# The masks of two attention stages added on TensorE, with the work at the ends of the stages in another order

## The reference

```
first block:  h += 0.5*ffn(norm h); h += conv mixer; h += 0.5*ffn;  kv projections of h
              h += 0.5*ffn; h += nsa(norm h) @ w_o; h += 0.5*ffn
   nsa: 16 heads, each with 3 branches (15 compressed keys, 256 selected, 256 in the window),
        softmax(q k^T / 8 + bias), gated and summed
second block: x += rms_norm(even_mixer(rms_norm x)) ; x += rms_norm(odd_mixer(rms_norm x))
   even: 8 heads of width 64 over the 64 best keys of an index score; retention beside it
   odd:  4 differential heads: softmax(q1 k1) - lambda softmax(q2 k2), and 8 latent heads of 96
         s = jnp.where(kpos <= qpos, q k^T * scale, -inf); p = softmax(s); o = p v
   m = concat(...) @ w_out (1024 x 1024); x = x + rms_norm(m, post_norm)
```

## Time and profile before

| | us |
|---|---|
| median of 3 runs | 1430.54 (1428.55 to 1437.21) |
| the profiled execution | 1427.65 |
| its span | 1425.4 |
| PE busy in it | 1305.7 (92%) |
| DVE busy | 889.0 (62%) |
| ACT busy | 619.0 (43%) |
| POOL busy | 438.4 (31%) |
| mean granted clock of PE | 0.961 |

### The profile page before, as it was taken

One profiled execution on the slowest core, in us unless ns is written; L12 is line 12 of the kernel. 1 busy time (PEld: TensorE's weight loads), 2 busy tenths in 40 slices (PEclk: granted clock), 3 DMA queues, 4 the chain that ended last, 5 costly groups with the idle time before them and its releaser, 6 DMA issues.

```text
span 1425.4 us, 27104 instructions
## 1 busy us (share of the span) xinstructions
PE 1305.7 (92%) x10681; PEld 1239.2 (87%) x10681; DVE 889.0 (62%) x1228; ACT 619.0 (43%) x924; POOL 438.4 (31%) x198
## 2 busy tenths in 40 slices
PE   5899999999999998999998778999999997699776
PEld 4899998989999998999996547999999996688665
DVE  3685458786545576454567864754556687674795
ACT  3444335344434445343345674533434445434451
POOL 1345432214443343444410332344340004300042
PEclk9999999999999999999998799999999999999898
DMA  6877754656776455665643103666653460444012
GB/s 195 218 212 218 224 180 134 178 176 203 224 212 204 158 175 173 198 200 178 187 126 101 34 23 115 199 188 191 205 163 107 146 215 31 136 136 150 12 46 73
DMA packets 275097, 222.50 MB, mean 156 GB/s; under 512 B 8082, under 2 KB 256422, under 8 KB 274908
## 3 DMA queue, kind: packets, MB, share of 16 engines
q1 hardware_dynamic: 272528, 215.59, 49.8%
q0 software_dynamic: 1344, 4.46, 1.6%
q10 hardware_dynamic: 1164, 1.62, 0.4%
HBM read 216.40 MB, written 4.19 MB: 155 GB/s over the span
## 4 chain that ended last, share of the span: by engine, by line
PE 72%; DVE 14%; ACT 7%; DMA 3%; issue 3%; POOL 1%; ACTq 0%; DVEq 0%; SPq 0%
PE psum L669 22%; PE psum L671 22%; PE psum L670 22%; DVE wal L1568 2%; ACT pbuf L1378 1%; ACT wah L1156 1%; DVE pbuf L1781 1%; DVE nmx L1783 1%; DVE hnl L1586 1%; POOL wbl L2172 1%; DVE wal L1742 1%; ACT wbh L1163 1%; ACT hnh L1226 1%; DMA raw_a<-in_ffn_w_in 1%; PE psum L632 1%
## 5 line engine op out<-in xcount | busy, mean ns | idle before, releaser
L669 PE MATMUL psum<-hnh,wah 128*128 128x256 f32 (+1 forms) x2080 | 589.9, 284 | 14.3 <-DVE wal L1568 7.7
L670 PE MATMUL psum<-hnl,wah 128*128 128x256 f32 (+1 forms) x2080 | 581.2, 279 | 0.0
L671 PE MATMUL psum<-hnh,wal 128*128 128x256 f32 (+1 forms) x2080 | 580.8, 279 | 0.0
L2172 POOL TENSOR_TENSOR wbl<-raw_b,wbh 128x1024 fp32r<-128x1024 f32 x114 | 369.0, 3238 | 570.6 <-ACT wbh L1163 465.0
L669 PEld LDWEIGHTS psum<-hnh,wah 128*128 128x128 f32 (+1 forms) x2080 | 396.3, 191 | 21.4 <-issue 8.6
L670 PEld LDWEIGHTS psum<-hnl,wah 128*128 128x128 f32 (+1 forms) x2080 | 395.8, 190 | 2.2 <-issue 1.7
L671 PEld LDWEIGHTS psum<-hnh,wal 128*128 128x128 f32 (+1 forms) x2080 | 395.8, 190 | 0.0
L1568 DVE TENSOR_TENSOR wal<-raw_a,wah 128x2048 fp32r<-128x2048 f32 (+1 forms) x129 | 298.0, 2310 | 105.4 <-ACT wah L1156 104.2
L1156 ACT ACTIVATE wah<-raw_a 128x2048 fp32r<-128x2048 f32 (+2 forms) x127 | 238.9, 1884 | 92.7 <-PE psum L671 65.4
L1264 ACT ACTIVATE gate_hid<-tmp 128x256 f32<-128x256 f32 x88 | 36.7, 417 | 421.0 <-DVE tmp L1677 421.0
L669 PE MATMUL psum<-hidh,wbh 128*128 128x256 f32 x768 | 213.3, 278 | 5.3 <-DVE hidl L1622 5.2
(11 more groups left out here) (286 smaller groups left out, 1568.7 us busy)
## 6 DMA issues: line engine op xcount, KB each, us to landing
raw_a<-in_ffn_w_in SPq DMA_DIRECT2D x176, 512.0 KB, 5.1
raw_b<-in_ffn_w_out SPq DMA_DIRECT2D x88, 512.0 KB, 5.0
raw_a<-in_w_in_even SPq DMA_DIRECT2D x15, 1024.0 KB, 5.4
raw_a<-in_conv_w_in SPq DMA_DIRECT2D x24, 512.0 KB, 3.9
raw_a<-in_w_in_odd SPq DMA_DIRECT2D x11, 1024.0 KB, 5.3
raw_a<-in_w_kv SPq DMA_DIRECT2D x6, 1024.0 KB, 6.5
raw_b<-in_conv_w_out SPq DMA_DIRECT2D x8, 512.0 KB, 5.6
raw_a<-in_attn_w_q SPq DMA_DIRECT2D x4, 1024.0 KB, 5.2
```

The source lines that it names most:

```text
L669: mm(dst, wh, xh, start=start, stop=False)
L670: mm(dst, wh, xl, start=False, stop=False)
L671: return mm(dst, wl, xh, start=False, stop=stop)
L2172: g.tensor_tensor(wbl[:, s], raw_b[:, s], wbh[:, s].bitcast(F32), ALU.subtract).then_inc(S("b_lo"), 1)
```

## The change

Masks: causal16, dmask and a 128 x 128 identity are kept in bf16. In even and odd PE first writes the mask into the score banks (identity times mask), then adds q k^T. DVE takes the maxima from PSUM and scales them; ACT takes the exps from PSUM with the scale in the instruction and writes the probabilities. The scores of duo g now wait for the exps of duo g-2. In nsa, ACT copies a unit's high part before the exps of the step, and DVE takes its low part one step later (back = LAG + 3); late_queries runs at steps 6, 9, 12, 15, and PE asks at 12, 15, 18, 21. Low parts of the last output row (even) and the last two (odd) go from POOL to DVE. The Sqrt table load of the even stage is made right after its attention stage, that of the odd stage is gone. DVE adds pairs of squares (half_ready), and PE sums four tiles instead of eight. At the end PE sums hres and the normed output in PSUM, both by a product with the identity, into four banks; ACT copies three of them, DVE one. Cut diff:

```diff
--- before.py
+++ after.py
@@ -148,6 +148,9 @@
         zero = sb("zero", [P, 512], BF16)
+        causal16 = sb("causal16", [P, 384], BF16)
+        dmask = sb("dmask", [P, 384], BF16)
+        ident16 = sb("ident16", [P, P], BF16)
         rms = sb("rms", [P, T + 2])
@@ -342,6 +344,9 @@
+        Y_BANK = (4, 5, 7, 6)
+        POOL_LOWS = {"nsa": 2, "even": 7, "odd": 6}
@@ -467,7 +472,10 @@
                 c = slice(half * 512, (half + 1) * 512)
-                sp.wait_ge(S("y_copied"), j + 1)
+                if j == 2:
+                    sp.wait_ge(S("y_third"), 1)
+                else:
+                    sp.wait_ge(S("y_copied"), min(j + 1, 3))
                 sp.dma_start(out[0, tt * P:(tt + 1) * P, c], xn[:, tt, c]).then_inc(S("y_stored"), 16)
@@ -570,7 +578,7 @@
-                                 bias=dmask[:, None, :].to_broadcast([P, 2, 384]), scale=SQRT_D,
+                                 bias=None, mask=dmask, scale=SQRT_D,
@@ -578,17 +586,16 @@
-            bias = causal[:, None, :].to_broadcast([P, 2, 384])
-                duos.append(dict(kind="full", q=[cq[r, h] for r in rows], k=[ck[r, h] for r in rows], bias=bias,
-                                 scale=SQRT_D, v=[v, v], rows=[slice(0, P)] * 2, coef="lambda", first=True, last=True,
+                duos.append(dict(kind="full", q=[cq[r, h] for r in rows], k=[ck[r, h] for r in rows], bias=None,
+                                 mask=causal16, scale=SQRT_D, v=[v, v], rows=[slice(0, P)] * 2, coef="lambda", first=True, last=True,
-                duos.append(dict(kind="full", q=[q96[0:96, h] for h in hs], k=[k96[0:96, h] for h in hs], bias=bias,
-                                 scale=96 ** -0.5, v=[[mv[:, t, h * 64:(h + 1) * 64] for t in range(2)] for h in hs],
+                duos.append(dict(kind="full", q=[q96[0:96, h] for h in hs], k=[k96[0:96, h] for h in hs], bias=None,
+                                 mask=causal16, scale=96 ** -0.5, v=[[mv[:, t, h * 64:(h + 1) * 64] for t in range(2)] for h in hs],
@@ -639,12 +646,12 @@
                 for j in range(4):
-                    n["sqn"] += 1
-                    pe.wait_ge(S("sqn_ready"), n["sqn"])
-                    for t in (2 * j, 2 * j + 1):
-                        m = mm(bank[6][:, 0:T], one1, sqm[:, t, :], start=t == 0, stop=t == KT - 1)
+                    n["half"] += 1
+                    pe.wait_ge(S("half_ready"), n["half"])
+                    m = mm(bank[6][:, 0:T], one1, sqm[:, 2 * j, :], start=j == 0, stop=j == 3)
                 m.then_inc(S("ss_ready"), 1)
                 n["rn"] += 1
+                n["sqn"] += 4
@@ -860,8 +867,15 @@
                         if g >= 2:
-                            pe.wait_ge(S("max_ready"), g - 1)
-                        if du["kind"] == "full":
+                            pe.wait_ge(S("max_ready" if name == "nsa" else "exp_ready"), g - 1)
+                        if du["bias"] is None:
+                            for i in range(2):
+                                mm(bank[x0 + i][:, 0:384], ident16[:, :], du["mask"][:, :], start=True, stop=False)
+                            for i in range(2):
+                                mm(bank[x0 + i][:, 0:T], q[i][:, P:T], k[i], start=False, stop=False)
+                            for i in range(2):
+                                x = mm(bank[x0 + i][:, T:384], q[i][:, 0:P], k[i][:, 0:P], start=False, stop=True)
+                        elif du["kind"] == "full":
                             for i in range(2):
@@ -991,8 +1005,8 @@
                     pe.wait_ge(S("rt_ready"), n["rn"])
-                elif st in (12, 18):
-                    pe.wait_ge(S("late_queries"), st // 6 - 1)
+                elif st in (12, 15, 18, 21):
+                    pe.wait_ge(S("late_queries"), st // 3 - 3)
@@ -1128,13 +1143,21 @@
                 half, tt = j // 2, j % 2
-                pe.wait_ge(S("res_ready"), 34 + 2 * half)
-                if j >= 2:
-                    pe.wait_ge(S("y_copied"), j - 1)
+                if Y_BANK[j] == 6:
+                    pe.wait_ge(S("rt_ready"), n["rn"])
+                open_bank(Y_BANK[j])
                 for t in range(4):
-                    x = pe.transpose(bank[4 + tt][:, t * P:(t + 1) * P],
-                                     hres[:, 4 * half + t, tt * P:(tt + 1) * P], ident)
-                x.then_inc(S("y_ready"), 1)
+                    mm(bank[Y_BANK[j]][:, t * P:(t + 1) * P], hres[:, 4 * half + t, tt * P:(tt + 1) * P], ident,
+                       start=False, stop=False)
+            for half in range(2):
+                for t in range(4):
+                    pe.wait_ge(S("y_part"), 4 * half + t + 1)
+                    for tt in range(2):
+                        x = mm(bank[Y_BANK[2 * half + tt]][:, t * P:(t + 1) * P],
+                               arena[:, 8 + 4 * half + t, tt * P:(tt + 1) * P], ident,
+                               start=False, stop=t == 3)
+                        if t == 3:
+                            x.then_inc(S("y_ready"), 1)
@@ -1208,7 +1231,6 @@
-                link(act.activation(lut[:, :], eps[:, :], ACT.Sqrt))
                 act.wait_ge(S("ss_ready"), n["rn"])
@@ -1367,22 +1389,25 @@
                         x.then_inc(S("pt_copied"), 1)
+                    if name == "nsa" and st >= LAG + 2 and duos[st - LAG - 2]["last"]:
+                        du = duos[st - LAG - 2]
+                        act.wait_ge(S("pv_done"), d0 + st - LAG - 1)
+                        act.activation(hnh[:, du["tile"], :], bank[4 + du["unit"] % 2][:, 0:T], ACT.Copy
+                                       ).then_inc(S("o_hi"), 1)
                     if st < M:
...
                             ((0, NC, 0), (NC, 2 * NC, 1))
+                        masked = duos[st]["bias"] is None
                         for m in range(2):
                             r, p = 2 * (g % ND) + m, probs(g)[:, m]
+                            src = bank[2 * (g % 2) + m] if masked else p
                             for lo, hi, i in cuts:
-                                x = act.activation(p[:, lo:hi], p[:, lo:hi], ACT.Exp,
+                                x = act.activation(p[:, lo:hi], src[:, lo:hi], ACT.Exp,
+                                                   scale=duos[st]["scale"] if masked else 1.0,
                                                    bias=nmx[:, r, i:i + 1], accum_out=sm[:, r, i:i + 1])
                         x.then_inc(S("exp_ready"), 1)
-                    if name == "nsa" and st >= LAG + 2 and duos[st - LAG - 2]["last"]:
-                        du = duos[st - LAG - 2]
-                        act.wait_ge(S("pv_done"), d0 + st - LAG - 1)
-                        act.activation(hnh[:, du["tile"], :], bank[4 + du["unit"] % 2][:, 0:T], ACT.Copy
-                                       ).then_inc(S("o_hi"), 1)
                     behind(st)
@@ -1483,6 +1508,7 @@
             attend("even")
+            load_root()
             mix_rest()
@@ -1531,6 +1557,11 @@
             root_residual(lambda j: bank[j][:, :], lambda j: act.wait_ge(S("acc_ready"), 4 * 7 + j + 1))
+            for j in (0, 1, 3):
+                half, tt = j // 2, j % 2
+                act.wait_ge(S("y_ready"), j + 1)
+                act.activation(xn[:, tt, half * 512:(half + 1) * 512], bank[Y_BANK[j]][:, :], ACT.Copy
+                               ).then_inc(S("y_copied"), 1)
@@ -1646,12 +1677,21 @@
-            def post_residual(g, following=None):
-                n["sqn"] += 4
+            def post_residual(g, following=None, last=False):
                 n["acc"] += 4
+                for j in range(4):
+                    n["sqn"] += 1
+                    v.wait_ge(S("sqn_ready"), n["sqn"])
+                    v.tensor_tensor(sqm[:, 2 * j, :], sqm[:, 2 * j, :], sqm[:, 2 * j + 1, :], ALU.add
+                                    ).then_inc(S("half_ready"), 1)
                 v.wait_ge(S("acc_ready"), n["acc"])
                 inverse_root(T)
+                if last:
+                    for t in range(KT):
+                        v.scalar_tensor_tensor(arena[:, 8 + t, :], acc(t), gains[:, g, t:t + 1], rstd[:, 0:T],
+                                               ALU.mult, ALU.mult).then_inc(S("y_part"), 1)
+                    return
                 for j in range(4):
@@ -1765,7 +1805,8 @@
                 M, d0, u0_ = len(duos), DBASE[name], UBASE[name]
-                for st in range(M + LAG + 2):
+                back = LAG + (3 if name == "nsa" else 2)
+                for st in range(M + back):
                     between(st)
@@ -1777,7 +1818,12 @@
                         p = probs(g)
-                        if du["kind"] == "full":
+                        if du["bias"] is None:
+                            v.reduce_max(nmx[:, r, 1], two_banks(x0, P, T), AX, negate=True)
+                            link(v.reduce_max(nmx[:, r, 0], two_banks(x0, P, 384)[:, :, T:384], AX, negate=True))
```

(42 more changed lines are left out.)

8 lines of the change are left out of this document (4 added, 4 removed).

## The result

| | before | after |
|---|---|---|
| median of 8 runs each, us | 1431.13 (1428.55 to 1437.8) | 1416.4 (1411.78 to 1423.89) |
| profiled execution, us | 1427.65 | 1413.42 |
| its span, us | 1425.4 | 1411.6 |
| PE busy, us | 1305.7 | 1311.3 |
| mean granted clock | 0.961 | 0.977 |

What follows compares the result with a forecast made beforehand. Three-part matmuls on PE, left alone, were taken to bound the kernel, so only PE's waits could pay. Terms -13.6 + 0 - 3.5 - 0.5 - 1.1 - 2.8 - 5.0 = -26.5 took 1427.65 to 1401.2 us; range 1397 to 1415.

Steps and rivals of the forecast that it cites:

- first stage: First attention stage (nsa): DVE's waits for ACT's copy vanish and query norms move later; -13.6 us, bounds -4 and -18.
- second stage: Second attention stage (even), masks on PE: four duos, a latency chain, so 0 us; bounds -1 and +4.
- rows and root, even: Even output matrix's last row on DVE, -0.5 us; residual's root with moved table load and paired squares, -2.8 us.
- third stage: Third attention stage (odd), masks on PE: DVE saves 0.7 us a duo at first, 0.3 later; -3.5 us in all.
- rows, odd: Last two rows of the odd output matrix go from POOL to DVE; -1.1 us.
- the end: Program's end: residual and normed output summed on PE by identity products; 18.3 us becomes 13.3, -5.0 us.
- the order of the copies: First attention stage: ACT copies before the exps, DVE takes it a step later; six waits removed, -11.6 us.
- late queries: First attention stage: four reciprocal-and-multiply pairs move to later steps, out of the loop's filling; -2 us, bounds 0 and 4.4.
- Rival 1: First attention stage: PE or ACT becomes the new bound, -4 us instead of -13.6; 1413.6 us, chance 0.17.
- Rival 2: Masks bring nothing: third attention stage 0, second +1 us; given as 1408.8 us, chance 0.10.
- rival 4: Second and third attention stages: PE falls to 1.2 GHz and stays; sum +12.6 us, 1443 us, chance 0.03.
- rival 3: Program's end: an identity product costs four transposes, so +3 us instead of -5; 1412 us, chance 0.04.

Runs made afterwards that it cites:

- masks_only: Kernel before with only the masks put on PE (16-bit masks, identity product, exps from the banks); profiled run 1430.44 us.
- order_only: Kernel before with only ACT's output copy ahead of the exps and DVE's evacuation a step later in the first attention stage; profiled run 1413.65 us.
- before_r2: Kernel before, unchanged, profiled a third time; profiled run 1441.35 us.
- first_stage: Kernel before with all edits of the first attention stage, the late query heads moved too; profiled run 1412.56 us, ratio 0.9935 in ten runs.
- late_undone: Kernel after with the late query heads back at steps 2, 4, 6, 8; 1413.68 us, ratio 0.983 to the kernel before.
- after_r4: Kernel after, unchanged, fifth profile and third comparison; 1419.23 against 1437.23 us, ratio 0.9893.
- roots_only: Kernel before with only the pairs of squares and the moved or dropped root table loads; profiled run 1430.49 us.
- drain: Kernel after with PE waiting once in each feed-forward loop step for its own product; 1455.64 us, ratio 1.0178 to the kernel before.

## Why the prediction missed

Stretches after the step of the prediction that each tests, medians of four and five profiles, us:

| step | forecast | measured |
|---|---|---|
| first stage | -13.6 | -12.1 (93.5 to 81.4); -14.0 in the first pair of profiles |
| second stage | 0 | -1.5 |
| rows and root, even | -0.5 - 2.8 | -1.4 |
| third stage | -3.5 | -4.0 |
| rows, odd | -1.1 | -1.1 |
| the end | -5.0 | -4.5 |
| sum | -26.5 | -24.6; -25.3 in the first pair |

**The step that failed** is the one beside which no number stands: "nearly all of the time is three-part matmuls that the change leaves alone", and so the sum was put on a profiled execution as if the other thousand microseconds would repeat. They don't: a long loop has two lengths, 5.4 to 6.7 us apart. By luck the profile of before had no slow loop; the one of after had two, 12.4 us of the 12.7 that the forecast of the span missed (13.8 for 26.5). For the medians (14.7) this scatter of what was left alone is the only cause that the runs show; whether the kernel after meets the slow pace oftener by its change stays open. The changed stretches came out within 2 us of their sum, in part since errors cancel: the order of the copies brought more than forecast, the late queries and the rows and root less. I could have seen it: the three runs of the kernel before spread over 8.7 us (1428.55 to 1437.21), and my range of 18 us held only the bounds of the changed steps.

**First stage.** The mechanism was right: the eight waits of the earlier trace rows became two at the very end, 4.1 us, where no later step of VectorE's loop is held up:

```profile
DVE hnl L1876 <- ACT hnh L1395: 4.1, 2, 2.5
```

The order was mis-sized, though: -14.2 for -11.6. A unit was to start every 8.1 to 8.5 us; it is 7.45 without queries and 9.87 with. Between the two rows VectorE is busy 7.12 of 9.86 us, so the wait of 1.72 was not its only idle time. Late queries -2: wrong sign, +1.4 or more. That their work "no longer falls where the loop is filling" was the error; filling is where VectorE had time. Rival 1, PE or ScalarE as the new bound at -4 us, did not come: PE is busy 62 of 80 us, at a clock of 0.89.

**Second stage.** Forecast 0, bound -1; measured -1.0 in the first pair and -1.5 by medians. The term took no account of the clock. Over all 18 profiles the length of this stage follows PE's granted clock in it: 18.6 to 18.9 us at 1.00, 19.4 to 19.8 at 0.91, 19.9 to 20.2 at 0.83, 20.6 to 21.0 at 0.75. The four profiles of before had 0.75 to 0.83, four of five of after 1.00. masks_only (19.6) and order_only (19.8) both had 0.91; which part lifts it to 1.00 no run shows, nor was the clock varied by itself.

**Third stage.** Forecast were periods of 2.8 us in the first four duos, and idle time of VectorE that ends on PE in the later ones. VectorE in the kernel after:

```profile
1345.87 0.68 DVE L1822 TENSOR_REDUCE nmx<-psum 128x2 f32<-128x512 f32 x1
...
1348.64 0.68 DVE L1822 TENSOR_REDUCE nmx<-psum 128x2 f32<-128x512 f32 x1
...
1356.50 0.69 DVE L1822 TENSOR_REDUCE nmx<-psum 128x2 f32<-128x512 f32 x1 [0.43 <-PE psum L877]
```

The period is 2.77 us, down from 3.56, and the idle time on PE is there. Rival 2 is out by the -4.0 us, rival 4 by the mean clock of 0.95. (By its own terms rival 2's time is 1408.5, not 1408.8.)

**Rows and root, even.** Forecast -3.3 in all, measured -1.4 (40.4 to 39.0 by medians). First the rows: they were to gain 0.5 and took 30.1 to 30.5 us in four of five profiles of after, for 28.3 to 28.6 in before. Waits for the seventh row in the kernel after, ScalarE first, then PE:

```profile
1219.18 1.06 ACT L1186 ACTIVATE wbh<-raw_b 128x1024 fp32r<-128x1024 f32 x1 [4.61 <-DMA raw_b<-in_w_out_even]
...
1222.81 0.36 PE L676 MATMUL psum<-hnh,wbh 128*128 128x256 f32 x1 [2.55 <-POOL wbl L2217]
```

The transfer of that row lands late: ScalarE waits 4.6 us for it, 2.7 in before. But the lateness is not what costs. The last two rows behind that wait, in after and then in before_r2, where the same row is as late (ScalarE waits 4.51, PE 2.46):

```profile
1222.80:1230.00 7.20, 7.19 (x49) 7.16 (x50) 4.26 (x4) 4.77 (x5) 0.00 (x0) 0.76 0.33 93
```

```profile
1238.30:1244.10 5.80, 5.73 (x48) 5.72 (x49) 2.29 (x1) 4.66 (x5) 2.28 (x1) 1.00 0.40 125
```

The second keeps a granted clock of 1.00 and its rows take 28.4 us in all; in the first PE fell to 1.2 GHz for 16 products. All seven profiles with rows of 30.1 to 30.5 us (first_stage, masks_only and late_undone too) have this low stretch, and none of the others has it. after_r4, the fifth profile of after, doesn't. Its last row waits for nothing, as forecast (0.53 us in before), but PE waits 0.9 us before the sixth where before has no wait, and the rows take 28.5 us: no gain either.

Then the root. Its square root starts 2.17 us behind the closing product instead of 5.47, and the next projection 8.7 us behind it instead of 12.0, in the four profiles with slow rows. That is more than the forecast 2.8, but only since these rows close later. With rows of 28.4 and 28.5 us (roots_only, after_r4) the projection comes 10.0 and 9.9 us behind, a gain of 2.1: in roots_only ScalarE works on the next mixer's first weights until 0.4 us before the closing product, and only then squares; VectorE adds the first pair at 1237.45, behind its own 2.29 us of work on these weights and 0.8 us later than the first square allows; PE's four products then take 1.97 us. The forecast had put only the last product behind the last square. Rows and root together are 38.4 and 38.5 us with quick rows and 38.8 to 39.2 with slow ones, so of the 1.8 us of longer rows 0.4 to 0.9 show. In first_stage and masks_only, with the table load still behind the weights, none of it does (40.6 us; 39.3 to 40.6 in before).

**The end.** Forecast 13.3 us from the closing product, measured 13.8. In the kernel after:

```profile
1397.96 2.01 PE L651 MATMUL psum<-arena,cst 128*128 128x256 f32 x8
1400.02 1.05 PE L1150 MATMUL psum<-cst,hres 128*128 128x128 f32 x8
1400.91 0.38 PE L681 MATMUL psum<-zero 128*128 128x512 bf16 x1
...
1402.49 3.22 DVE L1692 SCALAR_TENSOR_TENSOR arena<-psum,par,rstd 128x256 f32<-128x256 f32 x8
...
1404.23 3.74 PE L1156 MATMUL psum<-cst,arena 128*128 128x128 f32 x32
...
1407.78 0.69 DVE L2198 COPY arena<-psum 128x512 f32<-128x512 f32 x1 [2.07 <-PE psum L1156]
```

Eight product instructions count for four products, and the next bank is opened 0.89 us after they start: 0.22 us each, the price that was taken from the earlier trace rows, with PE without a gap and a clock of 1.00. A transpose took 0.21 us at the low clock, so about 0.11 at the full one: the product costs two of them, and rival 3 is out. The Trainium skill ("TensorE: Matmul & The Clock Gate", Terms) gives the transpose mode as four times faster for FP32; taken as against such a product, the trace does not agree. The 0.5 us that are missing lie mostly behind the last copy: it ends at 1408.61, and the span 3.0 us later where 2.6 had been put for the store.

## What to carry to other kernels

Before you add a forecast difference to one profile's time, ask what its unchanged part does from run to run: the spread of the runs belongs in the range, and the comparison is best made stretch by stretch, between events that both kernels have. An operation moved out of a loop's filling into its full flow costs its whole length where its engine is, or becomes, the bound. And behind a wait of PE look at its clock before you blame the wait: the same late row cost 7.20 us or 5.80 for what followed.

## What the runs showed of the hardware

A 128x256 product of this form with a weight load of its own starts 113.3 or 117.8 ns after the one before at a granted clock of 1.00 (2.4 GHz). In the drain run, as in the long loops, the pace held until PE waited. The slow pace makes 5.4 to 6.7 us on a loop of some 180.

The Trainium skill ("TensorE: Matmul & The Clock Gate", Wait — 56ns, not 53.3ns?) states one fixed addition of 2.5 ns to the columns' time once warm, which would be 109.2 ns, an estimate from that page for 256 columns; neither pace agrees (6.6 and 11.1 ns above the 106.7 of the columns alone).

A wait of PE for its own product costs 0.5 us a step (drain). Behind a wait of PE of about 2.5 us the granted clock fell in some executions of the same program and not in others; the 16 products at 1.2 GHz then cost some 1.5 us (1.7 us in the third projection, 1.4 in the last two rows of the second mixer).
